# Routing from the unnormalised x, a first gather in two parts, and expert weights in places outside the ring

## The reference

```python
x = x + memory_cross_attention(rms_norm(x, xattn_norm[l]), rms_norm(mem, mem_norm[l]), w_xq[l], w_xkv[l], w_xo[l])
x = x + hierarchical_moe(rms_norm(x, ffn_norm[l]), ...)

def rms_norm(x, g):
    return x * rsqrt(mean(x * x, axis=-1) + EPS) * g

# hierarchical_moe, h of (256, 1024)
pg = softmax(h @ w_rg + b_rg)                 # 4 groups, the best one is taken
le = (h @ w_re + b_re) of the chosen group    # 8 experts each, the best 2 are taken
w_top = softmax(the two) * pg(best)
y[t] += w_top * ((silu(gu[:, :512]) * gu[:, 512:]) @ w_e2[e]),   gu = h[t] @ w_e1[e]
```

## Time and profile before

| | |
|---|---|
| median of three runs | 1790.1 us |
| profiled execution | 1787.23 us, span 1784.8 us |
| PE busy | 1377.0 us (77%) |
| weight loads of PE | 1049.9 us (59%) |
| DVE busy | 603.5 us (34%) |
| ACT busy | 435.5 us (24%) |
| POOL busy | 107.5 us (6%) |
| DMA | 534.15 MB, mean 299 GB/s |
| mean granted clock of PE | 0.892 |

### The profile page before, as it was taken

The page is one execution under the profiler, slowest core; times in us unless marked ns, Lnnn a source line. Parts: engine busy times, 40 slices in busy tenths (PEclk is TensorE's granted clock), DMA queues, the critical chain, the costliest instruction groups (busy, mean ns, idle before and its releaser), DMA issues.

```text
span 1784.8 us, 30691 instructions
## 1 busy us (share of the span) xinstructions
PE 1377.0 (77%) x13324; PEld 1049.9 (59%) x13324; DVE 603.5 (34%) x865; ACT 435.5 (24%) x577; POOL 107.5 (6%) x29
## 2 busy tenths in 40 slices
PE   3999999889876766766657999988886755765765
PEld 3989999888733333334325999978843422422433
DVE  5758655644111001101004686566420100101002
ACT  5444544443200000000003545444210000000001
POOL 3501101024200000000000010010000000000000
PEclk7999999998988888888886999999888888887887
DMA  9463366434599999999998424662269999999994
GB/s 337 174 210 119 102 226 239 142 126 156 202 426 427 427 428 426 427 427 420 427 428 318 166 95 150 250 238 95 95 249 428 427 426 427 426 427 427 426 427 175
DMA packets 91939, 534.15 MB, mean 299 GB/s; under 512 B 9347, under 2 KB 12699, under 8 KB 65565
## 3 DMA queue, kind: packets, MB, share of 16 engines
q1 hardware_dynamic: 83592, 519.14, 72.2%
q10 hardware_dynamic: 8212, 13.00, 2.1%
HBM read 525.83 MB, written 6.29 MB: 298 GB/s over the span
## 4 chain that ended last, share of the span: by engine, by line
PE 43%; DMA 37%; issue 8%; DVE 8%; ACT 2%; ACTq 0%; POOL 0%; POOLq 0%; SPq 0%; DVEq 0%
DMA ring<-in_w_expert_out 34%; PE banks L1254 21%; PE banks L1558 5%; PE banks L1281 5%; PE banks L1532 3%; PE banks L1517 2%; DMA ring<-in_w_in 2%; PE banks L1569 2%; DMA ring<-in_w_expert_in 2%; DVE m_lo L814 1%; DVE hT L801 1%; DVE arena L1125 1%; PE banks L1415 1%; ACT w_hi L484 1%; DVE stat L798 1%
## 5 line engine op out<-in xcount | busy, mean ns | idle before, releaser
L1517 PE MATMUL banks<-ring,arena 128*32 128x256 f32 x4160 | 296.9, 436 | 147.5 <-DMA ring<-in_w_expert_in 142.5
L1517 PEld LDWEIGHTS banks<-ring,arena 128*32 128x32 f32 x4160 | 137.2, 122 | 288.2 <-DMA ring<-in_w_expert_in 181.0
L1254 PE MATMUL banks<-h_hi,w_hi 128*128 128x256 f32 x848 | 242.6, 286 | 2.4 <-DVEq L759 2.4
L1558 PE MATMUL banks<-ring,arena 128*32 128x256 f32 x2080 | 164.2, 469 | 100.8 <-DMA ring<-in_w_expert_out 87.1
L1254 PE MATMUL banks<-h_hi,w_lo 128*128 128x256 f32 x848 | 240.3, 283 | 0.0
L769 DVE TENSOR_TENSOR w_lo<-ring,w_hi 128x2048 fp32r<-128x2048 f32 (+1 forms) x90 | 185.0, 2055 | 145.4 <-ACTq L471 136.0
L1120 DVE TENSOR_TENSOR arena<-arena,banks 128x128 f32<-128x128 f32 x65 | 18.8, 289 | 593.2 <-ACT arena L726 592.7
L484 ACT CAST w_hi<-ring 128x2048 fp32r<-128x2048 f32 (+1 forms) x114 | 196.9, 1727 | 91.5 <-PE banks L1254 40.0
L1254 PE MATMUL banks<-h_lo,w_hi 128*128 128x256 f32 x720 | 204.1, 283 | 0.0
L726 ACT ACTIVATE arena<-banks 128x128 f32<-128x128 f32 x65 | 18.1, 278 | 737.6 <-PE banks L1517 737.6
L1558 PEld LDWEIGHTS banks<-ring,arena 128*32 128x32 f32 x2080 | 80.7, 130 | 163.1 <-issue 82.3
(11 more groups left out here) (277 smaller groups left out, 1955.8 us busy)
## 6 DMA issues: line engine op xcount, KB each, us to landing
ring<-in_w_expert_in SPq DMA_DIRECT2D x130, 2048.0 KB, 23.6
ring<-in_w_expert_out SPq DMA_DIRECT2D x65, 2048.0 KB, 24.7
ring<-in_w_in SPq DMA_DIRECT2D x24, 2048.0 KB, 8.9
...
```

The costliest lines, as they stand in the source:

```text
L1254: ins = pe.matmul(acc, stationary(a, k), moving(b, k), start=k == 0 and n == 0, stop=k == kc - 1 and n == 2)
L1517: ins = pe.matmul(G[32 * j:32 * j + 32, :], xTe[:, k, e * SL:(e + 1) * SL], w[:, k % 4, :, j * P:(j + 1) * P], start=k == 0, stop=k == KC - 1,
L1558: ins = pe.matmul(psum[32 * j:32 * j + 32, 5, 0:T], hhT[:, k * SL:(k + 1) * SL], w[:, k, j * T:(j + 1) * T], start=k == 0, stop=k == 3, ti ...
```

## The change

- `SPARE = (1, 3)`: of the units that follow the six of experts 0 and 1, the first layer keeps one and the second three in places outside the ring. Place 0 is a new buffer `spare_unit` (loaded right behind xq0); places 1 and 2 lie over `w_hi` and `hT` (second layer only; loaded when the last half of xo1 and the squares are done). In the second layer these are all three units of expert 2.
- Routing from raw x: PE transposes xT itself and multiplies it by router weights that DVE has scaled by the norm's weights (`wr_scaled`), two steps between the halves of xo1 and two behind them. ACT squares the transposed accumulators with a running sum (`accum_out`), so the root is of a 128x1 column for each token block. The root's inverse scales htok in ACT's copies and the logits on DVE. The norm's weights are applied when the gathered tokens are copied (`gff`, loaded by two more DMAs on ACT's queue). `norm2` and its parts go.
- Order in the first layer: the router stands ahead of xk and xv, `memory_low` behind the choice of experts; the opening of the four `moe` banks moves behind xv.
- First turn: `EARLY = 2` experts are gathered first (64 columns), then expert 0 and 1 run, then the other six are gathered (192 columns). Copies by ACT are eight for each gather, not four. The small tables' steps move behind experts 0 and 1.
- `dynamic_dma_scratch_size=1024`.

```diff
 NEG = -1e30
 R = 6
 UNIT = 4096
+SPARE = (1, 3)
 EI = 8
+EARLY = 2
...
-   ("xpt", 2, 2), ("xpv", 2, 2), ("xo", 4), ("norm2", 1), ("moe", 4)])
-ROUTER_JOBS = [("router", 1), ("htok", 4)]
+   ("xpt", 2, 2), ("xpv", 2, 2), ("xo", 3), ("htok", 2), ("xo", 1, 3), ("htok", 2, 2), ("router", 1)])
 K_JOBS, V_JOBS = [("xk", 4)], [("xv", 4)]
     for layer in range(L):
         order += jobs(layer, ([("norm0", 1)] if layer else []) + MIX_JOBS)
-        order += jobs(layer + 1, K_JOBS) if layer + 1 < L else []
-        order += jobs(layer, ROUTER_JOBS)
-        order += jobs(layer + 1, V_JOBS) if layer + 1 < L else []
-        order += jobs(layer, [("place", 1), ("start", 1), ("table", 1)])
+        order += jobs(layer + 1, K_JOBS + V_JOBS) if layer + 1 < L else []
+        order += jobs(layer, [("moe", 4), ("place", 1), ("start", 1), ("table", 1)])
     order += jobs(L, [("norm0", 1), ("out", 4)])
     bank_of = {"moe": None, "place": 4, "start": 5, "table": 5}
...
+        spare_loaded = [sem(f"spare_loaded{i}") for i in range(3)]
+        def expert_place(layer, n):
+first = n < R
+if R <= n < R + SPARE[layer]:
+    return None, n - R
+u = FIRST_EXPERT[layer] + n - (0 if first else SPARE[layer])
+return u, u % R
...
+            if layer:
+                sp.wait_ge(S["units_used"], 3 * NE * (layer - 1) + R + 1)
+            sp.dma_start(spare_units[0], w1[R // 3, R % 3]).then_inc(spare_loaded[0], 16)
     for name in KV_UNITS if layer + 1 < L else []:
         load_dense(layer + 1, name)
     u0 = FIRST_EXPERT[layer]
...
+    def spare_load(i):
+        n = R + i
+        expert_unit(spare_units[i], n // 3, n % 3, spare_loaded[i])
     for n in range(R):
-        slot_is_free(u0 + n)
-        expert_unit((u0 + n) % R, n // 3, n % 3, slot_loaded[(u0 + n) % R])
+        ring_unit(n)
+        if n == R - 1 and SPARE[layer] > 1:
+            sp.wait_ge(S["acc_ready"], piece_job(layer, "xo1", 1)[1])
+            spare_load(1)
+            sp.wait_ge(S["ssq_ready"], 4 * (layer + 1))
+            spare_load(2)
+    head = R + SPARE[layer]
+    for n in range(head, head + R):
+        ring_unit(n)
     with sp.Fori(0, TURNS - 1) as turn:
-        for n in range(R, R + 3 * EI):
+        for n in range(head + R, head + R + 3 * EI):
+            _, slot = expert_place(layer, n)
             sp.wait_ge(S["units_used"], turn * (3 * EI) + (3 * NE * layer + n - R + 1))
-            expert_unit((u0 + n) % R, turn * EI + n // 3, n % 3, slot_loaded[(u0 + n) % R])
...
 n_norm, n_x = [1], [0]
+def token_roots(layer):
+    for j in range(4):
+        acc = job_wait(act, layer, "htok", j)
+        post(act.activation(hT[:, 2 * (j % 2):2 * (j % 2) + 2, :], two(acc), ACT.Square, accum_out=ssq[:, j:j + 1]), "ssq_ready")
+    act.wait_ge(S["ssq_biased"], layer + 1)
+    for tb in range(TB):
+        post(act.activation(rms_tok[:, tb:tb + 1], ssq[:, 2 + tb:3 + tb], ACT.Sqrt, bias=ssq_bias[:, tb:tb + 1],
+                            scale=1.0 / D), "rms_ready")
+    n_x[0] += 1
...
     act.dma_start(lnt[:, 1, :], A["gmlp_ln_b"][layer:layer + 1].broadcast_to([P, MW])).then_inc(S["ln_loaded"], 16)
     act.dma_start(bs[0:1, :], A["gmlp_b_s"][layer].rearrange("g i -> (g i)").unsqueeze(0)).then_inc(S["ln_loaded"], 16)
+    for l in range(L) if layer == 0 else ():
+        act.dma_start(gff[:, l, :].rearrange("p (h k) -> p h k", h=2),
+                      A["ffn_norm"][l].rearrange("(h p k) -> p h k", h=2, p=P)).then_inc(S["gff_loaded"], 16)
...
         act.wait_ge(S["mhat_loaded"], 16)
         memory_high(layer + 1, mhatT)
-    x_norm(layer, "norm2", False)
+    link(act.activation(small[:, 58:59], small[:, 95:96], ACT.Sqrt))
+    token_roots(layer)
+    act.wait_ge(S["rstd_ready"], layer + 1)
+    for j in range(4):
+        half, tb = j // 2, j % 2
+        acc = job_wait(act, layer, "htok", j)
+        post(act.activation(htok[:, tb, half * 512:half * 512 + 512].rearrange("t (k p) -> t k p", k=4),
+                            acc.rearrange("t (p k) -> t k p", k=4), ACT.Copy, scale=rstd_tok[:, tb:tb + 1]), "htok_ready")
+        act.sem_inc(free(layer, "htok", j), 1)
+    def router_exps():
+        act.wait_ge(S["r_shift"], layer + 1)
+        link(act.activation(rt[:, 20, 0:8], rt[:, 20, 0:8], ACT.Exp))
+        post(act.activation(rt[:, 21, 0:2], rt[:, 21, 0:2], ACT.Exp), "r_exp")
...
-    act.wait_ge(S["r_shift"], layer + 1)
-    link(act.activation(rt[:, 20, 0:8], rt[:, 20, 0:8], ACT.Exp))
-    post(act.activation(rt[:, 21, 0:2], rt[:, 21, 0:2], ACT.Exp), "r_exp")
-    if layer + 1 < L:
+        make_k(layer + 1, router_exps)
         make_v(layer + 1)
-    def experts(Q, turn, ne):
+    else:
+        router_exps()
+    act.wait_ge(S["gff_loaded"], 32)
+    def gathered(Q, count, e0, e1, banks):
+        n = (e1 - e0) * SL
+        for r in range(4):
+            act.wait_ge(Q["gathered"], count + (r + 1))
+            for c in range(2):
+                k = 2 * r + c
+                bank, at = banks(k)
+                act.activation(xTe[:, k, e0 * SL:e1 * SL], psum[:, bank, at:at + n], ACT.Copy,
+                               scale=gff[:, layer, k:k + 1]).then_inc(Q["xe_ready"], 1)
...
-            act.wait_ge(Q["gathered"], turn * 4 + (r + 1))
-            act.copy(xTe[:, 2 * r:2 * r + 2, 0:ne * SL],
-                     psum[:, (7, 5)[r % 2], :].rearrange("p (c s) -> p c s", c=2)[:, :, 0:ne * SL]).then_inc(Q["xe_ready"], 1)
+        if early:
+            gathered(Q, count - 4, 0, early, lambda k: ((7, 6, 5, 7)[k // 2], k % 2 * T))
         for e in range(ne):
+            if e == early:
+                gathered(Q, count, early, ne, lambda k: ((7, 6)[k // 2 % 2], k % 2 * T))
...
     post(dve.tensor_tensor(flat(yb_lo), flat(uT), flat(yb_hi).bitcast(F32), ALU.subtract), "y_ready")
+    dve.wait_ge(S["wr_loaded"], 32 * (layer + 1))
+    post(dve.tensor_tensor(wr[:, :, :], wr[:, :, :], bc(vec[:, layer, ROW_FF:ROW_FF + KC], NG + NE), ALU.mult), "wr_scaled")
...
         split_to(layer, f"xo{i // 2}", i % 2)
         if i == 3:
-            pair_sums(0, 1)
+            dve.wait_ge(S["ssq_ready"], 4 * layer + 2)
+            post(dve.tensor_scalar(ssq_bias, ssq[:, 0:2], 1.0 / D, EPS, ALU.mult, ALU.add), "ssq_biased")
         add_x(layer, "xo", i)
-    pair_sums(2, 3)
-    if layer + 1 < L:
-        memory_low(layer + 1, mhatT)
-    norm(ROW_FF, layer, False)
+    dve.wait_ge(S["rms_ready"], 2 * (layer + 1))
+    post(dve.reciprocal(rstd_tok, rms_tok), "rstd_ready")
     acc = job_wait(dve, layer, "router")
-    link(dve.tensor_tensor(logit[:, :, :], acc[:, 0:TB * (NG + NE)].rearrange("p (t n) -> p t n", t=TB),
-                           rbias[:, layer:layer + 1, :].broadcast_to([P, TB, NG + NE]), ALU.add))
+    for tb in range(TB):
+        link(dve.scalar_tensor_tensor(logit[:, tb, :], acc[:, tb * (NG + NE):(tb + 1) * (NG + NE)], rstd_tok[:, tb:tb + 1],
+                                      rbias[:, layer, :], ALU.mult, ALU.add))
...
     first_max(lem, NE, t1, oh1, wi)
     link(dve.scalar_tensor_tensor(lem, oh1, 2 * NEG, lem, ALU.mult, ALU.add))
     first_max(lem, NE, t2, oh2, wi)
-    link(dve.tensor_tensor(rt[:, 21, 0:2], t2, t1, ALU.subtract))
-    dve.sem_inc(S["r_shift"], 1)
     post(dve.tensor_tensor(mask[:, :, :], oh1, oh2, ALU.add), "mask_ready")
+    link(dve.tensor_tensor(ex, gl, bc(gm, NG), ALU.subtract))
+    post(dve.tensor_tensor(rt[:, 21, 0:2], t2, t1, ALU.subtract), "r_shift")
+    if layer + 1 < L:
+        memory_low(layer + 1, mhatT)
...
     dense_by_parts(layer, "xo0", "xo", o, lambda i: pe.wait_ge(S["o_ready"], 4 * layer + i + 1))
-    dense(layer, "xo1", "xo", o, i0=2)
-    norm(layer, "norm2")
+    def x_part(i):
+        pe.wait_ge(S["x_ready"], 4 + 12 * layer + 4 + i + 1)
+    def turn_x(i):
+        for tb in range(TB):
+            acc = tok_acc[2 * (i // 2) + tb]
+            for k in (2 * i, 2 * i + 1):
+                ins = pe.transpose(acc[:, (k % 4) * P:(k % 4 + 1) * P], xT[:, k, tb * P:(tb + 1) * P], ident)
+            if i % 2:
+                done(ins)
+    def route(i):
+        for k in (2 * i, 2 * i + 1):
+            for tb in range(TB):
+                ins = pe.matmul(router_acc[:, tb * (NG + NE):(tb + 1) * (NG + NE)], xT[:, k, tb * P:(tb + 1) * P], wr[:, k, :],
+                                start=k == 0 and tb == 0, stop=k == KC - 1, skip_group_check=True)
+        return ins
+    dense(layer, "xo1", "xo", o, i0=2, halves=(0,))
+    pe.wait_ge(S["wr_scaled"], layer + 1)
+    tok_acc = [job_begin(pe, layer, "htok", j) for j in range(2)]
+    router_acc = job_begin(pe, layer, "router")
+    x_part(1)
+    turn_x(0)
+    turn_x(1)
+    route(0)
+    route(1)
+    dense(layer, "xo1", "xo", o, i0=2, halves=(1,))
+    tok_acc += [job_begin(pe, layer, "htok", j) for j in range(2, 4)]
+    x_part(2)
+    turn_x(2)
+    route(2)
+    x_part(3)
+    turn_x(3)
+    done(route(3))
...
+        def gather(r, e0, e1, banks):
+            n = (e1 - e0) * SL
+            for k in (2 * r, 2 * r + 1):
```

(35 more changed lines are left out.)

148 lines of the change are left out of this document (76 added, 72 removed).

## The result

The changed kernel takes 1769.72 us (median of 4, 1769.31 to 1770.25) against 1790.55 us of the kernel before, run beside it (median of 4): ratio 0.9885, 95% interval 0.9871 to 0.990, so 20.8 us faster. The forecast was 1766.5 us, range 1756 to 1778. In the profiled executions the spans fall from 1784.8 to 1767.5 us, by 17.3. The rest of the 20.8 is not in the traces: the profiled execution of before lies 3.3 us under its median and that of after only 0.4, and outside its span it has 2.4 us against 1.8.

What follows compares the result with a forecast made beforehand. Bound by DMA streaming of expert weights at about 427 GB/s. Second layer 14.7 + 10.4 - 4.2 = 20.9 us plus first layer 4.9 - 0.2 - 2.0 = 2.7 us saves 23.6 us: 1766.5 us, range 1756 to 1778.

Steps and rivals of the forecast that it cites:

- Fewer units: Expert weight streams: one unit leaves the first layer's plateau and three the second's, gaining 4.9 and 14.7 us.
- Second layer: Units 14.7, earlier stream start 10.4, less 4.2 us lost to a gap: 20.9 us gained.
- I take eight at each level: 5.4 us: Second layer's two-expert gather: eight products at half clock and eight at full, 5.4 us, bounds 3.5 and 7.1.
- I take 4.2 us: Second layer's plateau: gap in the weight stream after six loads, 4.2 us, bounds 1 and 10.
- First layer: One unit 4.9 us, chain to the first release -0.2, start -2.0: 2.7 us gained.
- The start: Two norm-weight loads on ACT's queue ahead of the first cast: 2.0 us lost, bounds 0.8 and 6.0.
- My V end (468.6): First layer: V ends at 468.6 us, from 464.86 plus 9.0 for later low-part products, less 5.3 for router and transposes gone.
- A: Rival: half clock through experts 1 and 2, gap eats the second layer's three units; about 1775 us; chance 0.17.
- B: Rival: more gain, with no gap, DVE not blocked and start costing 0.8 us; 33.1 us gained, 1757 us; chance 0.15.
- C: Rival: earlier routing mostly eaten, narrow gathers at half clock throughout, ACT's two loads 6.0 us; 1775.6 us; chance 0.07.
- D: Rival: ring starves in both layers' first turns, run at 1.2 GHz; 22 us slower, 1812 us; chance 0.04.
- E: Rival: spare loads land late or delay dense weights, so the plateau keeps its units; within 0.2%; chance 0.02.

Runs made afterwards that it cites:

- the two experiments: The two ffn_norm loads moved behind the memory values' load in the changed kernel, 1764.3 us; the same loads added to the kernel before, 1795.2 us.
- the insert behind xo1: Changed kernel with the first two parts' transposes and router products moved from between the halves of xo1 to behind them: 1767.8 us.

## Why the prediction was right, and where it was not

The time came 3.2 us above the forecast and inside its own range (1761 to 1772). In spans I had -23.6 and got -17.3, so by the traces the sum was 6.3 us too high: 4.9 in the first layer and 1.8 in the tail, less 0.4 in the second layer. That the time is nearer is luck of the executions that were profiled. Step by step:

**Fewer units: right.** 4.9 and 14.7 us; taking all four away cost 18.4, two of them 7.1, as worked out with the gap.

**Second layer: right by two errors that cancel.** Counted from the start of its x projections, the logits came at 1282.7 (forecast 1283.5) and the gather at 1291.6 (1292.4). Then "I take eight at each level: 5.4 us" failed: all ran at 0.50, 7.06 us, most of the first expert's product too, and the release came at 1302.1 instead of 1300.1. Against it "I take 4.2 us" for the gap was too much: 2.1. The seventh load went out 31.6 us behind the first release, where the sum had 32.5 before the 1.2 us added for the clock. 14.7 + 8.7 - 2.1 = 21.3 us; forecast 20.9. The 8.7 is what is left over; by the releases it is 6.15 at the first and 2.2 for the closed gap, 8.4.

**First layer: wrong in its sign.** Forecast +2.7, measured -2.2. The first release came at 488.00 us where the sum, with its 2.0 us for the start, had 482.6: 5.4 us, of which 0.5 were won back behind it. Two terms make 3.3 and 2.7 of them, and 0.6 were won in between:

- The start: 5.3 us instead of "2.0 us lost". The queue was 2.4 us longer, ScalarE came to it 1.5 us later, which lies within the scatter of the traces, and a stretch at clock 0.93 followed. By the two experiments the loads cost the kernel 4 to 5 us in all.
- The gather and the product ahead of the release: 2.7 us by the half level, as in the second layer.

Two more errors cancel. My V end (468.6) took K and V, from the end of the eight low products on, in 45.9 us, as at full clock. But PE had done next to nothing for 13 us and ran K's first 5 us at 0.50, and K and V took 48.6: 2.7 us more. Against it K needs only the first of the eight low products, and started 43.65 us behind the x projections where I had 46.8: 3.2 us less. So V ended 0.4 us early by that measure.

The mechanism ahead of K was as said, blocked by POOL for 4.46 us; the blocked operation was the shift and not the first m_lo product, which makes no difference. What I passed by is that this step was a choice: moving m_lo ahead of the routing takes 13.6 us off, more than any error in my sum.

The Trainium skill (SBUF — State Buffer, section "SBUF: two separate sides") says that of a VectorE operation with two SBUF inputs and a GpSimd operation that reads SBUF the one that starts first holds the shared port pair for its whole instruction. The trace agrees: POOL started at 418.87, VectorE at 418.92, and a 128x2 operation ended with POOL's, at 423.4.

**The tail.** I took it as unchanged; it was 1.8 us longer. The last expert's second product took 3.25 us at clock 0.50 to 0.68, against 1.93 at 1.00 before. The change does not fix this: with the insert behind xo1 the kernel ended 50.9 us behind its last issue, the changed kernel 52.7, and eight kernels with the changed routing had the shorter tail.

**The rivals.** A (the gap eats the units): no. B (more than forecast): no, there was a gap and VectorE was blocked. C (the earlier routing mostly eaten: both gathers at half clock throughout, the loads at 6.0) had the two events and not their sum; it gave them 0.07, and each by itself was what happened. D: no, the queue stood empty for 2.1 us. E: no.
